# A hybrid RWKV/convolution backbone on one core: the key scale's exponential in front of the variance logarithms

## The reference

```python
def rwkv_inputs(z, w0, w_up, a0, a_up, k_k, k_a):
    ...
    kk = to_heads(k * k_k)
    kk = kk * lax.rsqrt(jnp.maximum(jnp.sum(kk * kk, -1, keepdims=True), 1e-24))
    ...
def rwkv_output(y, r, k, v, gz, gn_g, gn_b, r_k, g_up, w_out, dtype):
    B, T = y.shape[:2]
    yn = _standardize(y, GN_EPS).reshape(B, T, RWKV_DIM) * gn_g + gn_b
    ...
```

## Time and profile before

| | |
|---|---|
| median of 3 runs | 4037.71 us (4033.7 to 4046.82) |
| the profiled execution | 4042.05 us, its span 4040.2 us |
| mean granted clock of TensorE | 0.980 |
| TensorE busy | 3832.9 us, 95% of the span |
| VectorE, ScalarE, GpSimd busy | 1684.2, 1136.4, 552.0 us (42%, 28%, 14%) |
| ACT_TABLE_LOAD | 106 instructions, 136.0 us, 1283 ns each |

### The profile page before, as it was taken

How to read it: one execution, slowest core, us unless ns; L and a number is a source line. 1 busy time by engine, 2 the same in 40 slices (tenths; PEclk the granted TensorE clock), 3 DMA queues, 4 the chain that set the end, 5 groups by cost and what they waited for, 6 DMA issues and landing times.

```text
span 4040.2 us, 112746 instructions
## 1 busy us (share of the span) xinstructions
PE 3832.9 (95%) x51864; PEld 2572.9 (64%) x51864; DVE 1684.2 (42%) x2721; ACT 1136.4 (28%) x2003; POOL 552.0 (14%) x436
## 2 busy tenths in 40 slices
PE   7899999999999999999999989999999999999998
PEld 3666666666555555655555656666666556678887
DVE  2656656654872111322231255555555422132232
ACT  3544454542122000200000244444444221020001
POOL 0000000000032121122232100000000023314443
PEclk8999999999999999999999999999999999999999
DMA  5000000000333222211111310000010253242223
GB/s 207 25 9 25 25 25 25 30 18 28 103 134 99 94 94 94 85 52 63 56 59 63 127 42 9 24 24 24 24 34 21 88 187 110 84 143 92 84 91 129
DMA packets 76341, 277.46 MB, mean 69 GB/s; under 512 B 8672, under 2 KB 13024, under 8 KB 75488
## 3 DMA queue, kind: packets, MB, share of 16 engines
q1 hardware_dynamic: 67968, 235.96, 17.6%
q10 hardware_dynamic: 6624, 29.04, 1.9%
q0 software_dynamic: 1280, 5.24, 0.3%
HBM read 256.58 MB, written 13.63 MB: 67 GB/s over the span
## 4 chain that ended last, share of the span: by engine, by line
PE 89%; ACT 4%; issue 3%; DVE 2%; DMA 1%; POOL 0%; ACTq 0%; DVEq 0%; SPq 0%; POOLq 0%
PE psum L1177 17%; PE psum L1691 16%; PE psum L759 11%; PE psum L1058 11%; PE psum L1488 9%; PE psum L1623 6%; PE psum L1583 3%; PE psum L1070 3%; PE psum L1646 2%; PE psum L1209 2%; PE psum L1018 2%; PE psum L750 2%; PE psum L1126 1%; DMA ring<-w_stream_in 1%; PE psum L1036 1%
## 5 line engine op out<-in xcount | busy, mean ns | idle before, releaser
L1177 PEld LDWEIGHTS psum<-arena 32*32 32x32 f32 (+3 forms) x40512 | 702.7, 118 | 366.6 <-issue 281.4
L1177 PE MATMUL psum<-arena 32*32 32x32 f32 (+4 forms) x40512 | 795.4, 209 | 117.5 <-issue 85.1
L1058 PE MATMUL psum<-arena,ring 128*128 128x512 f32 (+1 forms) x1408 | 564.8, 523 | 5.5 <-ACT arena L1879 1.9
L759 PE MATMUL psum<-arena,ring 128*128 128x512 f32 (+1 forms) x1264 | 463.2, 524 | 3.8 <-DVE arena L2577 3.8
L759 PEld LDWEIGHTS psum<-arena,ring 128*128 128x128 f32 x1264 | 238.8, 191 | 230.4 <-issue 200.8
L1691 PE MATMUL psum<-arena 128*128 128x384 f32 (+1 forms) x1344 | 368.6, 433 | 0.0
L1058 PEld LDWEIGHTS psum<-arena,ring 128*128 128x128 f32 x1408 | 243.9, 192 | 133.3 <-issue 105.0
L1691 PEld LDWEIGHTS psum<-arena 128*128 128x128 f32 x1344 | 255.4, 190 | 106.4
L1691 PE MATMUL psum<-arena,ring 128*128 128x384 f32 (+1 forms) x1008 | 278.5, 433 | 0.0
L3016 POOL DMA_DIRECT2D ya_spill<-arena x16 | 8.8, 551 | 1957.5 <-DVE arena L2577 1957.5
L1691 PEld LDWEIGHTS psum<-arena,ring 128*128 128x128 f32 x1008 | 191.5, 190 | 79.6
(11 more groups left out here) (177 smaller groups left out, 4482.7 us busy)
## 6 DMA issues: line engine op xcount, KB each, us to landing
ring<-w_stream_in SPq DMA_DIRECT2D x440, 512.0 KB, 3.8
x_spill<-arena ACTq DMA_DIRECT2D x2, 3072.0 KB, 8.7
arena<-x_spill ACTq DMA_DIRECT2D x16, 384.0 KB, 6.7
arena<-ya_spill ACTq DMA_DIRECT2D x6, 768.0 KB, 6.0
ring<-w_stream_in ACTq DMA_DIRECT2D x8, 512.0 KB, 5.9
arena<-x_in ACTq DMA_DIRECT2D x1, 3072.0 KB, 14.5
arena<-ups_in SPq DMA_DIRECT2D x16, 192.0 KB, 2.5
ya_spill<-arena POOLq DMA_DIRECT2D x8, 384.0 KB, 5.6
```

Source lines behind the costliest of these rows:

```text
L759: mm = eng.matmul(psum[0:lhs[k].shape[-1], tile, a - off:b - off], lhsT=lhs[k], rhs=rhs[k][:, a:b], start=(k == 0), stop=(k == len(lhs) - ...
L1058: mm = pe.matmul(bank(j, z=b - a), lhsT=w[k], rhs=hs[k][:, a:b], start=(k == 0), stop=(k == KT - 1))
L1177: return pe.matmul(out, lhsT=lhs, rhs=rhs, start=start, stop=stop, skip_group_check=True)
```

## The change

ScalarE's exponential of the key norm (L1931, L1929 in the new file) is moved ahead of the two variance logarithms. Since the logarithms need the other table, each of the turns 2 to 7 of both layers gets two more table loads: 24 in all. On VectorE, two strings of `WEAVE` move a letter p one place forward past an s.

```diff
-WEAVE.update((("V", 0, t), "ttssssttsstssstsssstpstsspssssspssspssssppspssppsppsssspssssppppppsppssssptstsssstsssspspstspspsstp") for t in range(2, KT))
+WEAVE.update((("V", 0, t), "ttssssttsstssstsssstpstsspssssspssspssssppspssppsppsssspsssppsppppsppssssptstsssstsssspspstspspsstp") for t in range(2, KT))
...
                         act.activation(slot(kr(g, 1, 1)), slot(kr(g, 1, 1)), ACT.Ln, scale=float(2 ** LN_SHIFT)).then_inc(kkl.sem, 1)
                         yield
-                    yield from variance_log(0)
-                    yield from variance_log(1)
                     if prep:
                         tables(EXP)
                         act.wait_ge(*kkl.at(g))
                         act.activation(slot(kr(g, 1, 1)), slot(kr(g, 1, 1)), ACT.Exp, scale=-0.5, bias=eps_c(3)).then_inc(kke.sem, 1)
                         yield
+                    yield from variance_log(0)
+                    yield from variance_log(1)
```

More of the change, by code:

```diff
@@ L202 @@
 WEAVE.update((("V", 1, t), "tssstttsstssssssspsspssppssssppsssspsssppstsspsspspppssspppspspsspppspssspsssssssssssssss") for t in (1,))
-WEAVE.update((("V", 1, t), "tssssttstssssssststssspssssspsspspssssspsppsppspspssssssspppppppssssptspssstsssspsspsstspsspt") for t in range(2, KT))
+WEAVE.update((("V", 1, t), "tssssttstssssssststssspssssspsspspssssspsppsppspspsssssspsppppppssssptspssstsssspsspsstspsspt") for t in range(2, KT))
 WEAVE.update((("V", 1, t), "stssttsssttssssssssstssssssspspssssstsssstsptsssssspsppsppsssppspsssppsssssspssspspsp") for t in (KT,))
```

## The result

| | before | after |
|---|---|---|
| median | 4042.01 us (4 runs, 4033.7 to 4046.82) | 4096.66 us (4 runs, 4093.49 to 4098.63) |
| span of the profiled execution | 4040.2 us | 4094.9 us |
| mean granted clock of TensorE | 0.980 | 0.975 |

The ratio is 1.0128 (95% interval 1.0111 to 1.0146): the change makes the kernel 55 us slower, where 37 were predicted. The time lies above the predicted range, and ScalarE's 24 added loads are only a small part of it.

A forecast was written before the change was run, and what follows sets the result against it. TensorE carries 89% of the chain of waits, but the edited stretch's chain is ScalarE's. Layer 0's stall 19.5, layer 1's 12.1 and the clock's 5.4 make 37.0 us; 4037.7 + 37.0 = 4075 us, 8-in-10 range 4054 to 4092.

The forecast's parts named there:

- What bounds the kernel: TensorE carries 89% of the chain of waits; in the edited stretch, from L1951 to store L2060, the chain is ScalarE's.
- The stall: Layer 0: TensorE's second variance product waits 3.06 us a turn for the moved first logarithm; with 1.2 extra, 19.5 us.
- The free early piece: Layer 0, before L2034: added load and exponential need 2.14 of 2.40 us, free in turns 4 to 7.
- the 5.4 us that would be left without a stall: Layer 0: ScalarE's own added work alone, 0.7 per turn plus 1.2 for turns 2 and 3.
- The clock: Layer 0, behind the stall: TensorE's granted clock falls, slowing six wide rows; 0.9 us a turn, 5.4 in all, spread 0 to 10.8.
- Layer 1, 12.1 us: Both added loads stand before L1939; L1951 moves 2.7 us, less gaps before L2050: 1.6 in turn 4, 2.1 in five others.
- VectorE at 0: Key scaling L2528 moves ahead of L2663: free in layer 0, covered by a longer wait in layer 1; counted at 0.
- Only ScalarE's own work counts: Rival: the second variance product does not stall or is covered; layer 0 costs 5.4, total 17.5 us, 4055; chance 0.10.
- A load costs twice: Rival: ScalarE stands empty around each load for as long again; 31 us more at most, 4106; chance 0.04.
- Given back: Rival: turns end in a wait that does not move, swallowing most lateness; up to 10 us left, 4045; chance 0.06.
- faster: Rival: the next turn waits for VectorE and earlier scaling helps; at most 15.4 us gained, 4022; chance 0.03.

The follow-up runs named there:

- the added products in the kernel before: Kernel before with 20 added products in front of TensorE's second variance product in layer 0's turns: 4069.66 us, ratio 1.0074.
- the pair with the added products: Six added products in turns 2 to 7 of layer 1: in the kernel before 4046.99 us, with the change in layer 1 alone 4057.13 us.
- the first logarithm in front: Changed kernel, but layer 0's first logarithm keeps its old place, exponential between the logarithms, layer 1's ScalarE order as before: 4055.07 us, ratio 1.0043.
- the later product: Changed kernel with TensorE's second variance product one place later, behind a projection row and the 96 small products: 4061.11 us, ratio 1.0052.

## Why the prediction missed

**What bounds the kernel, and the direction**: right. The price of the added products in the kernel before (28.6 us for 28 us of work) shows TensorE as the bound of this stretch.

**The stall, 19.5 us for layer 0**: right in place, cause and size. Six stalls, 19.3 us together, all released by L1897; with the earlier ends counted they are 3.75 and 3.92 in turns 2 and 3 and 3.15 in the others, where 3.55, 3.75 and 3.06 were worked out. The free early piece (L2034 still waits 0.71) and the 5.4 us that would be left without a stall (6.2) are right too.

**The clock, 5.4 us with a spread of 0 to 10.8**: this is the step that failed. It measured 3.15 us in turn 4, against 0.9 taken and an upper bound of 1.8, and 16 to 20 us over the layer. Four things were wrong in it.
- The bound counted only the six wide rows, at 0.3 each, from the earlier trace rows. The low clock began with the stalled product itself and took the 96 small products too: 0.44 + 1.06 + 1.65. The small ones were left out without a row that speaks for it, and their 1.06 is more than the whole 0.9.
- The 0.3 was too low as well. It comes from four rows in 3.07 us, but these began at 618.09 and the clock fell only at 618.8 (the granted clock is 1.00 from 617.4 to 618.7 and 0.51 from 618.8 to 622.2), so they ran in part at the full clock. In turn 5 of the kernel after, six rows at 1.2 GHz throughout took 5.49 us instead of 2.84: 0.44 more each. A fall could cost 4.31 us a turn and did so three times, where 1.8 was the bound.
- "I take the middle, since the wide rows are about half of the work behind the stall" halves a bound that already left the other half out. And the lower bound, that "its low stretch falls on other work", did not come about: the low stretch of 6.8 us in turn 4 begins with the stalled product itself, and in turn 6, where it begins 1.8 us later, the rows behind the product still lost 1.67 us.
- The one precedent in the trace, 1.49 us of idle time and then 0.50, was half as long as the new stall, and a spread from no fall to a fall every time was taken from it. The runs showed a fall behind six stalls of six. In turns 2 to 7 the lateness gained was 4.5 to 8.8, in none of them the 3 of a bare stall.

With 3.15 a turn the sum would have been 19.5 + 12.1 + 18.9 = 50.5 and the time 4088; inside the range, with the result 9 us above it. 4.3 of the 9 is the kernel before, which came out at 4042.0 beside the changed one instead of 4037.7; the rest is as much as the 4.2 us by which layer 1's trace (16.3) lies over its 12.1, though one trace does not show that it is the same.

**Layer 1, 12.1 us**: the mechanism is right in turn 4 (L1951 2.83 us later after L2034, predicted 2.7; waits of 0.84 + 0.58 = 1.4 in turn 4, predicted 1.6). The size is 18 us by the run of layer 1 alone, 12 by the pair with the added products, 16.3 in the trace of the change, where 0.97 of granted clock became 0.96. But the untouched layer 1 of the kernel before with 20 products is at 0.96 too (2440 to 3180 us). "I take nothing" for the clock may have been too little here as well; that stays open.

**VectorE at 0**: right within some 10 us, by the run with its order undone.

**The rivals.** *Only ScalarE's own work counts* was worked out at 4055; the kernel that removes the stall is at 4061. Its mechanism was sound, and its condition ("if the product does not stall") is what one line on TensorE's side makes true. *A load costs twice* falls: 12 loads in layer 0 with the first logarithm in front cost 17 us, of which 14 were worked out without a drain, and 24 loads with the later product 20. By the Trainium skill ("ScalarE: Activation LUTs", What ACT_TABLE_LOAD costs) 24 loads would take an estimated 24 x 2.66 = 64 us of ScalarE; the trace agrees with its 1283 ns and shows nothing of the 1380 ns of drain. *Given back* and *faster* fall by the result.

## What to carry to other kernels

Price a new wait on the engine that sets the end in two parts: its length, and what the clock costs on everything queued behind it, small products too. Here each stall of 3 us cost about 6. When such a wait can't be avoided, look first at the waiting engine's own queue for an independent piece that can stand in front of it (here 35 of 55 us for a move of one step), and only then at filler, which returned the clock's half and kept the stall's. And measure a layer's small differences over several executions, since the falls of the clock move from one to the next: an untouched layer came out up to 14 us later.

## What the hardware did that was not expected

- 32 x 32 products take 1.71 us per 96 at 2.4 GHz and 2.77 at 1.2 GHz (a factor of 1.6; the six wide rows go from 2.84 to 5.49 when all of them run at 1.2 GHz, a factor of 1.9). The prediction had left the small ones out of the clock's price, and they slow with the clock all the same.
- Idle times of 0.92 and 1.00 us, some 3 us apart, left the clock at full; one of 2.99 us brought it down right behind. In between the length alone does not decide: 1.49 us in turn 5 of the kernel before were followed by a fall, 1.47 us at 868.46 in turn 7 of the kernel after were not (granted clock 1.00 from 867 to 878).
- Products of a constant with itself, 2.84 us of them in a stall of some 3 us, keep the clock up for the work behind it.
- An ACT_TABLE_LOAD between two activations that need different tables takes 1.30 us from its start to the next start, in every place where the new order put one. It costs a little more than that: L1939 came 0.69 us behind L2044 before (520.91 and 520.22) and 2.11 us behind it after (539.00 and 536.89), 1.42 more, since the two no longer overlap.
